# The last layer of the filter network as stacked high and low halves in fp32r, and its first block placed later

## The reference, cut to what matters

```
h = sin(freq * (z @ w1 + b1)); h = sin(freq * (h @ w2 + b2)); h = sin(freq * (h @ w3 + b3))
h = h @ w4                     # (512, 64) @ (64, 2048)
h = h * exp(-t * deltas)       # a decay for each of the 2048 columns
```

## Time and profile before

| what | value |
|---|---|
| median of three executions | 1481.8 us |
| the profiled execution | 1482.13 us |
| its span in the trace | 1480.2 us |
| TensorE busy | 1456.6 us, 98% of the span |
| VectorE, ScalarE, GpSimd busy | 824.7, 620.5, 323.1 us |
| TensorE on the chain that ended last | 90% |

### The profile page before, as it was taken

The page is one execution under the profiler, slowest core; times in us unless marked ns, Lnnn a source line. Parts: engine busy times, 40 slices in busy tenths (PEclk is TensorE's granted clock), DMA queues, the critical chain, the costliest instruction groups (busy, mean ns, idle before and its releaser), DMA issues.

```text
span 1480.2 us, 17827 instructions
## 1 busy us (share of the span) xinstructions
PE 1456.6 (98%) x7004; PEld 1190.7 (80%) x7004; DVE 824.7 (56%) x1240; ACT 620.5 (42%) x1000; POOL 323.1 (22%) x305
## 2 busy tenths in 40 slices
PE   9999999999999999999999999999999999999998
PEld 7776668888878888888888878877788888888887
DVE  6456666444576553554457447777757544345434
ACT  6545763233453322444345336564435333123332
POOL 1363221102032200121015312136531111111102
PEclk9999999999999999999999999999999999999999
DMA  8351106654264544365327221235513333323321
GB/s 272 112 176 51 57 29 208 218 171 155 95 223 144 174 150 157 126 206 184 125 100 252 68 77 65 72 101 168 190 64 120 100 100 100 100 86 100 100 85 58
DMA packets 54607, 189.97 MB, mean 128 GB/s; under 512 B 6584, under 2 KB 7385, under 8 KB 54395
## 3 DMA queue, kind: packets, MB, share of 16 engines
q1 hardware_dynamic: 48442, 167.06, 34.2%
q0 software_dynamic: 4880, 17.30, 3.5%
q10 hardware_dynamic: 1200, 4.46, 0.8%
HBM read 176.20 MB, written 12.60 MB: 128 GB/s over the span
## 4 chain that ended last, share of the span: by engine, by line
PE 90%; ACT 4%; DVE 4%; issue 1%; DMA 0%; POOL 0%; SPq 0%; ACTq 0%; DVEq 0%
PE PS L470 88%; PE PS L483 2%; ACT TMP L1270 1%; ACT TMP L1268 1%; ACT wh L1172 0%; DVE TMP L1835 0%; DMA X<-in_x 0%; ACT TMP L1283 0%; DVE TMP L2286 0%; DVE HTl L2369 0%; DVE wl L1787 0%; ACT TMP L1692 0%; ACT HTh L1194 0%; DVE HTl L1803 0%; ACT HTh L1685 0%
## 5 line engine op out<-in xcount | busy, mean ns | idle before, releaser
L1787 DVE TENSOR_TENSOR wl<-raw,wh 128x1024 fp32r<-128x1024 f32 x208 | 271.2, 1307 | 316.9 <-ACT wh L1172 316.7
L470 PE MATMUL PS<-HTh,wh 128*128 128x512 f32 (+1 forms) x1072 | 417.9, 390 | 2.6 <-POOL HTl L2688 1.1
L470 PE MATMUL PS<-HTl,wh 128*128 128x512 f32 (+1 forms) x1072 | 414.1, 387 | 0.0
L470 PE MATMUL PS<-HTh,wl 128*128 128x512 f32 (+1 forms) x1072 | 411.1, 386 | 0.0
L1172 ACT ACTIVATE wh<-raw 128x1024 fp32r<-128x1024 f32 x228 | 239.4, 1053 | 272.7 <-PE PS L470 268.0
L470 PEld LDWEIGHTS PS<-HTh,wh 128*128 128x128 f32 x1072 | 201.4, 188 | 49.9 <-issue 7.8
L470 PEld LDWEIGHTS PS<-HTh,wl 128*128 128x128 f32 x1072 | 200.3, 188 | 41.0
L470 PEld LDWEIGHTS PS<-HTl,wh 128*128 128x128 f32 x1072 | 201.5, 188 | 39.1 <-DVE HTl L1803 0.7
L470 PE MATMUL PS<-wh,FFh 128*128 128x512 f32 (+1 forms) x442 | 170.2, 385 | 0.0
L470 PE MATMUL PS<-wh,FFl 128*128 128x512 f32 (+1 forms) x442 | 169.9, 384 | 0.0
L470 PE MATMUL PS<-wl,FFh 128*128 128x512 f32 (+1 forms) x442 | 169.9, 384 | 0.0
(11 more groups left out here) (339 smaller groups left out, 2106.1 us busy)
## 6 DMA issues: line engine op xcount, KB each, us to landing
raw<-in_ws SPq DMA_DIRECT2D x268, 512.0 KB, 3.8
taps<-TMP SPq DMA_DIRECT2D x16, 256.0 KB, 2.4
tab<-in_spec POOLq DMA_DIRECT2D x8, 512.0 KB, 5.1
raw<-taps SPq DMA_DIRECT2D x8, 512.0 KB, 3.7
kd<-TMP POOLq DMA_DIRECT2D x16, 256.0 KB, 6.5
wh<-in_wd POOLq DMA_DIRECT2D x8, 512.0 KB, 4.0
wl<-in_wd POOLq DMA_DIRECT2D x8, 512.0 KB, 4.7
kf<-kd SPq DMA_DIRECT2D x8, 512.0 KB, 4.2
```

The costliest lines, as they stand in the source:

```text
L470: return nc.tensor.matmul(out, l, r, start=start, stop=stop, skip_group_check=True)
L1787: tt(WL[k][:, :n], RAW[RAW_AT["unit", u, 0] % RAWS][:, :n], f32(WH[k][:, :n]), ALU.subtract).then_inc(sem("lo_dve"), 1)
```

## The change

- The weights `w4` are now loaded whole on both halves of the partitions: 64 rows x 2048 columns, twice, 1 MB in place of 512 KB. The load stands ahead of weight unit 4 in SyncE's queue, without a wait, and has a semaphore of its own.
- ScalarE makes the high part `W4h` with two copies of 128 x 1024 in its `second(0)`, before the first sine. GpSimd makes the low part `W4l` (in place of `W4`) with two subtractions of 128 x 1024, each as soon as ScalarE's copy is there.
- After the last sine ScalarE copies the upper half of the features into `FTh` and the lower half, rounded, into `FTr`. VectorE subtracts and puts the low part of the features into the upper half of `FTr`. So `FTr` holds the high parts of the 64 features on partitions 0 to 63 and their low parts on 64 to 127.
- A tap block is now four fp32r products of full height: for each direction `FTr` with `W4h`, and `FTr` with `W4l`.
- TensorE's tap block 0 moves from `second(3)` into `first(4)`, between the `gmv` steps and the first `qk` group. VectorE's part of it moves into its `first(4)` as well, behind the low parts of two weight units.

The core of the diff:

```diff
-        W4 = at("w4", 168, [P, D])
+        W4, W4h, W4l = at("w4", 136, [P, 2, D]), at("w4h", 0, [P, 2, D], F32R), at("w4l", 136, [P, 2, D], F32R)
+        FTr, FTh = (at("ft", 176 + 2 * k, [P, S], F32R) for k in (4, 5))
...  tensor_program, first(4)
                             token_step("gmv", kk, 2048, 256, "p_gmv")
+                        taps(0, 0)
...  tensor_program, taps
-                e.wait_ge("f_sin", 3)
-                e.wait_ge("d_w4", 48)
+                e.wait_ge("ft_hi", 2)
+                e.wait_ge("ft_lo", 1)
+                e.wait_ge("w4_lo", o + 1)
                 for d in range(2):
-                    pr = slice(64 * d, 64 * d + 64)
-                    mm(PS[:, BANK["tap", n + d], :], TMP[pr, 4, i * P:(i + 1) * P], W4[pr, o * S:(o + 1) * S], True,
-                       True).then_inc(sem("p_tap"), 1)
+                    b, x, c = BANK["tap", n + d], FTr[:, i * P:(i + 1) * P], slice(d * S, d * S + S)
+                    mm(PS[:, b, :], x, W4h[:, o, c], True, False)
+                    mm(PS[:, b, :], x, W4l[:, o, c], False, True).then_inc(sem("p_tap"), 1)
...  scalar_program, second
+                    if k == 0:
+                        e.wait_ge("d_w4r", 16)
+                        for o in range(2):
+                            act(W4h[:, o, :], W4[:, o, :], ACT.Copy).then_inc(sem("w4_hi"), 1)
                     e.wait_ge("f_red", 7 * k + 7)
                     act(T((4, 5, 4)[k]), T(3), ACT.Sin).then_inc(sem("f_sin"), 1)
+                    if k == 2:
+                        e.wait_ge("f_sin", 3)
+                        act(FTh[64:128, :], TMP[64:128, 4, :], ACT.Copy).then_inc(sem("ft_hi"), 1)
+                        act(FTr[0:64, :], TMP[0:64, 4, :], ACT.Copy).then_inc(sem("ft_hi"), 1)
...  vector_program, first(4): taps(0, 0) after weights(...); second(3):
+                    e.wait_ge("ft_hi", 1)
+                    tt(FTr[64:128, :], TMP[64:128, 4, :], f32(FTh[64:128, :]), ALU.subtract).then_inc(sem("ft_lo"), 1)
...  gpsimd_program, behind weights(1)
+            for o in range(2):
+                e.wait_ge("w4_hi", o + 1)
+                tt(W4l[:, o, :], W4[:, o, :], f32(W4h[:, o, :]), ALU.subtract).then_inc(sem("w4_lo"), 1)
...  sync_program
+            engine.dma_start(W4[:, :, :], a["hy_w4_2"].rearrange("p (o c) -> p o c", o=2)).then_inc(sem("d_w4r"), 16)
             weights(SLOTS - 2)
...
-            engine.dma_start(W4[:, :], a["hy_w4_2"]).then_inc(sem("d_w4"), 16)
```

More of the change, by code:

```diff
@@ L636, in second @@
                     filter_layer(k)
-                elif k < 11:
+                elif 3 < k < 11:
                     taps(*divmod(k - 3, 2))
@@ L1234, in second @@
                     if o == 0:
-                        e.wait_ge("d_w4", 48)
+                        e.wait_ge("d_w4", 32)
                         if i:
@@ L1870, in second @@
                     filter_layer(k)
+                elif k == 3:
+                    e.wait_ge("ft_hi", 1)
+                    tt(FTr[64:128, :], TMP[64:128, 4, :], f32(FTh[64:128, :]), ALU.subtract).then_inc(sem("ft_lo"), 1)
                 elif k < 11:
@@ L2992 @@
         "lam": np.concatenate([i[n].reshape(-1) for n in ("lam_q1_2", "lam_q2_2", "lam_k1_2", "lam_k2_2")]),
-        "hy_w4_2": i["hy_w4_2"][0].reshape(64, 2, 2, S).transpose(2, 0, 1, 3).reshape(P, D),
+        "hy_w4_2": np.tile(i["hy_w4_2"][0].reshape(64, 2 * D), (2, 1)),
     }
```

## The result

| | before | after |
|---|---|---|
| median of 20 runs each | 1481.7 us | 1484.16 us (1482.93 to 1485.08) |
| ratio | | 1.0015, 95% interval 1.0009 to 1.0022 |
| profiled execution | 1482.13 us | 1484.52 us |
| span; mean granted clock | 1480.2 us; 0.997 | 1482.5 us; 0.996 |

The change makes the kernel 2.5 us slower, 0.15%. That is inside the range and inside what was called no change, but the way there is not the forecast's alone.

What follows compares the result with a forecast made beforehand. TensorE bounds the kernel, with a sine chain through VectorE and ScalarE from 20.8 to 40.3 us. 1482.13 + 4.15 (late sine) - 0.88 (block 0) - 2.5 (seven blocks) = 1482.9, as median 1482.6 us; range 1478.5 to 1485.7.

Steps and rivals of the forecast that it cites:

- The step that decides: GpSimd beside VectorE before the first sine: they take turns on shared SBUF ports, making the sine 4.15 us late.
- chain of three: VectorE's three dependent L1835 instructions ahead of the first sine, 22.48 to 24.63 us, each with both inputs in SBUF.
- The open point, who is next: Which engine gets the ports when one waits and the other has a successor; bounds nothing to 4.15 us.
- at 1049 us: Trace place where GpSimd and VectorE took turns; a VectorE instruction of a 0.72 us form took 2.89.
- at 49 us: Trace place where two VectorE subtractions ran back to back, 2.34 us for both, and GpSimd waited for both.
- The products: Tap blocks on TensorE: four products of 0.227 us each; seven blocks gain 2.5 us, block 0 net 0.88.
- Load, copies on ScalarE, features: W4's larger load, ScalarE's two copies before the first sine and the feature split after the third: each priced zero.
- full cover: Rival: none of GpSimd's work meets VectorE's chain; 3.4 us faster, 1478.4 us; chance 0.10.
- the sum: Main forecast from the profiled execution: 1482.13 + 4.15 - 0.88 - 2.5 = 1482.9, as median 1482.6 us; chance 0.45.
- The clock falls: Rival: TensorE's 3.9 us idle before filter layer 1 lowers its clock behind 30 us; +2.9, 1485.5 us; chance 0.27.
- VectorE keeps the ports: Rival: GpSimd waits out VectorE's chain, about 2 us lost at filter layer 2; 1480.4 us; chance 0.13 with one turn.
- It does not do what it says: Rival: W4 lands late or new products cost up to today's block; 2 to 5 us slower than the sum; chance 0.05.

Runs made afterwards that it cites:

- one-half experiment: The changed kernel with only the second of GpSimd's two subtractions held back until the third sine; 1481.05 us, ratio 0.9994 to before.
- first experiment: The changed kernel with both GpSimd subtractions for W4l held back until the third sine is done; 1478.23 us, ratio 0.9974 to before.
- busy-stall experiment: The changed kernel with 30 unread 128 x 128 transposes on TensorE ahead of filter layer 1; 1482.38 us, ratio 1.0003 to before.
- subtractions-alone kernel: The kernel before with only two unread GpSimd subtractions of 128x1024 added, released after ScalarE's silu; 1487.93 us, ratio 1.0036 to before.

## Why the prediction was right, and where not

**The step that decides was read rightly.** GpSimd's subtractions, released by the copies, met the chain of three. The prediction had two instances near 2.8 us; they took 2.77 and 2.72. It had the first sine at 29.27 and TensorE idle 3.9 us; they came to 28.97 and 3.6. Of the sine's 0.30, 0.25 is that VectorE's chain began that much earlier in this profile (22.23 and not 22.48); the two turns cost 4.10 us (6.25 - 2.15) where the prediction had 4.15. The Trainium skill's "SBUF — State Buffer" ("Who interferes with whom") says that the one without the ports waits for a whole instruction. The trace is near that: 2.77 us for a form of 0.70 is a wait of 2.07, where a subtraction of GpSimd's is recorded with 2.37. The open point, who is next, went as at 1049 us and not as at 49 us: in the gaps of the dependent chain GpSimd came in. That the gap is what lets it in is inferred; no experiment varied the gap alone. The one-half experiment priced a turn at 2.07 us.

**The products.** 0.23 us each; seven blocks gave 2.63 for 2.5 predicted, block 0 gave 1.80 and took 0.95, net 0.85 for 0.88 predicted. **Load, copies on ScalarE, features:** nothing to be seen, as argued; the first experiment has them all and starts its filter layers at 26.30 and 33.11, where before had 26.22 and 33.06. Its time, 1478.23, is what the prediction gave for full cover, 1478.4.

**The step that failed** is the one that was not in the sum: that TensorE's clock would stay at 1.00 behind the stall. I had that as the rival *The clock falls*, at 0.27, and held against it that no row showed a plain pause of this length, only one of narrow products. The busy-stall experiment shows that the pause does it, and the one-half experiment that even 1.6 us can, where I had said that it decides at about 4. So the forecast's case by itself, 1481.5 to 1483.7, missed the 1484.16; the range held it because it reached to the rival, and the number is right for that reason and not by the sum. The rival's price of 2.9 us measured 2.7 in the trace and 1.8, with over 1 us of uncertainty, in the medians; its 1485.5 was 1.3 too much. Against the profiled execution (1482.9 + 2.9 = 1485.8, measured 1484.52) the ledger splits the same 1.3: filter layer 1 was 3.44 late and not 3.83 (0.4, of which 0.24 lay ahead of the stall), the clock with filter layer 2 came to 3.09 and not 3.2 (0.1), the seven blocks gave 0.1 more, and the late fall of the earlier trace rows, which no step speaks of, was short in this profile and long in that of before (0.7 with the wait behind it and what else lies behind 103 us). The rivals *VectorE keeps the ports*, *Full cover* and *It does not do what it says* did not happen.

The chances had the outcome among no change by the bound of 0.2%. With 20 runs the measurement tells more: the kernel is slower, by 0.09 to 0.22%.

## What to carry to other kernels

Work that is given to an engine because it is idle there must be asked what it shares with the engine that is not: here 5.4 us of GpSimd's idle time cost 5.9 us of the kernel, and one wait that put the same work behind VectorE's dependent chain turned a loss of 2.5 us into a gain of 3.7. Price a stall of TensorE as its length and, behind it, a stretch at the lower clock; if the stall can't be moved, work that nobody reads holds the clock up. And when a block's operands get a longer preparation, look at where the block stands before looking at what it costs: the same products at their old place, with their operands split behind the last sine, were 9 us slower.

## What the runs showed that I had not expected

- A pause of 1.6 us behind a dense stream was enough to bring the clock down for 3.4 us in the traced run, and the times of this one kernel fall in two groups, with medians of 1480.05 and 1481.47 us. Behind 3.6 us it was down 6.8 us in one kernel and 3.4 in another.
- 128 x 128 transposes of a constant, 13 or 30 of them, hold the clock at 1.00. 32 products of one column do not: the clock fell while they ran, at 985.5.
- A VectorE `tensor_scalar` with one input in SBUF, 0.43 us otherwise, took 2.50 us beside GpSimd's subtraction (L1833 in the subtractions-alone kernel). Being held is no matter of two SBUF inputs alone.
- VectorE's subtraction for the features, half the partitions and 512 columns, took 2.72 us beside GpSimd (L1882 above). It took 0.69 after the change, and 2.77 in the first experiment, where nothing was in a hurry for it.
